# Opening of a two-block transformer kernel: vectors laid out by the host, two modulation chunks multiplied on TensorE, window bias and rope angles moved into the opening

## The reference, cut to what matters

```
cond = silu(c)
mod = cond @ w_mod[l] + b_mod[l]              # 1024 x 9216 per layer
sh1, sc1, g1, sh2, sc2, g2, sh3, sc3, g3 = split(mod, 9)
h = rms_norm(x, norm_g) * (1 + sc1) + sh1     # before each sub-layer
x = x + 0.5 * g1 * swiglu(h, w_gu, w_down)

rel  = pos[query] - pos[key]                  # window attention, 128 wide
bias = rel_bias[t5_bucket(rel)]               # 32 buckets x 6 heads
ang  = pos * 10000 ** (-arange(16) / 16)      # rope of the latent attention
```

## Time and profile before

| what | us |
|---|---|
| median of 3 runs (2005.84 to 2014.0) | 2006.38 |
| the profiled execution, as timed | 2002.22 |
| its span, first to last instruction | 2000.4 |
| PE busy | 1839.9 (92%) |
| DVE busy | 1425.0 (71%) |
| ACT busy | 932.1 (47%) |
| first matmul of the first strip | 66.19 after the start |
| first mixer, from its x_stats to the next | 264.34 to 431.88 |
| the same stage of the second layer | 822.65 to 972.23 |

### The profile page before, as it was taken

One profiled execution on the slowest core, in us unless ns is written; L12 is line 12 of the kernel. 1 busy time (PEld: TensorE's weight loads), 2 busy tenths in 40 slices (PEclk: granted clock), 3 DMA queues, 4 the chain that ended last, 5 costly groups with the idle time before them and its releaser, 6 DMA issues.

```text
span 2000.4 us, 24149 instructions
## 1 busy us (share of the span) xinstructions
PE 1839.9 (92%) x9068; PEld 1490.0 (74%) x9068; DVE 1425.0 (71%) x1956; ACT 932.1 (47%) x1480; POOL 137.2 (7%) x264
## 2 busy tenths in 40 slices
PE   1699986789999999978999999999999999999997
PEld 0577865678887888767788878787878788877886
DVE  5668788767887788676778776567787765567554
ACT  1444344664445444655643364345433544445443
POOL 2011100001110111000011000000111000000000
PEclk9999998889999999986999999999999999999999
DMA  6789823049885898331589865445998563447552
GB/s 243 262 293 340 313 97 127 22 149 329 309 311 197 314 322 324 124 118 42 186 306 336 298 214 187 136 163 171 329 321 299 200 221 128 172 147 271 194 186 86
DMA packets 242299, 439.48 MB, mean 220 GB/s; under 512 B 16201, under 2 KB 156551, under 8 KB 241927
## 3 DMA queue, kind: packets, MB, share of 16 engines
q1 hardware_dynamic: 204810, 304.75, 45.2%
q0 software_dynamic: 36320, 131.13, 17.4%
q10 hardware_dynamic: 1052, 2.06, 0.3%
HBM read 436.79 MB, written 1.09 MB: 219 GB/s over the span
## 4 chain that ended last, share of the span: by engine, by line
PE 73%; DVE 14%; DMA 5%; ACT 5%; issue 3%; SPq 0%; DVEq 0%; ACTq 0%
PE bank L1592 22%; PE bank L1594 21%; PE bank L1593 21%; DVE weights_lo L972 4%; DMA arena<-in_w_ada 2%; DMA arena<-in_w_mod 2%; PE bank L1755 1%; DVE mod_acc L996 1%; DVE arena L1088 1%; DMA weights_raw<-in_w_ffn_gu 1%; DVE x L1152 1%; DVE arena L1146 1%; ACT weights_hi L561 1%; DMA weights_raw<-in_w_ffn_in 1%; DVE hT_lo L1097 1%
## 5 line engine op out<-in xcount | busy, mean ns | idle before, releaser
L972 DVE TENSOR_TENSOR weights_lo<-weights_raw,weights_hi 128x1024 fp32r<-128x1024 f32 (+2 forms) x584 | 672.6, 1199 | 175.6 <-ACT weights_hi L561 175.4
L1592 PE MATMUL bank<-weights_hi,hT_hi 128*128 128x512 f32 x1760 | 699.0, 397 | 31.6 <-DVE hT_lo L1097 20.0
L1594 PE MATMUL bank<-weights_hi,hT_lo 128*128 128x512 f32 x1760 | 686.6, 390 | 0.0
L1593 PE MATMUL bank<-weights_lo,hT_hi 128*128 128x512 f32 x1760 | 685.5, 389 | 0.0
L561 ACT ACTIVATE weights_hi<-weights_raw 128x1024 fp32r<-128x1024 f32 (+2 forms) x584 | 572.1, 1037 | 141.2 <-PE bank L1594 84.0
L1592 PEld LDWEIGHTS bank<-weights_hi,hT_hi 128*128 128x128 f32 x1760 | 332.9, 189 | 115.1 <-issue 27.9
L1594 PEld LDWEIGHTS bank<-weights_hi,hT_lo 128*128 128x128 f32 x1760 | 332.2, 189 | 69.7
L1593 PEld LDWEIGHTS bank<-weights_lo,hT_hi 128*128 128x128 f32 x1760 | 333.3, 189 | 64.0
L996 DVE SCALAR_TENSOR_TENSOR mod_acc<-arena,silu_cond,mod_acc 128x1024 f32<-128x1024 f32 x198 | 254.0, 1283 | 61.8 <-DMA arena<-in_w_mod 28.1
L704 ACT ACTIVATE actT_hi<-bank 128x512 fp32r<-128x512 f32 x66 | 39.5, 599 | 490.7 <-PE bank L1755 490.7
L1592 PE MATMUL bank<-weights_hi,actT_hi 128*128 128x512 f32 (+1 forms) x544 | 214.3, 394 | 7.4 <-DVE weights_lo L972 7.4
(11 more groups left out here) (277 smaller groups left out, 1312.2 us busy)
## 6 DMA issues: line engine op xcount, KB each, us to landing
weights_raw<-in_w_ffn_gu SPq DMA_DIRECT2D x176, 512.0 KB, 5.7
arena<-in_w_mod POOLq DMA_DIRECT2D x144, 512.0 KB, 6.6
weights_raw<-in_w_in SPq DMA_DIRECT2D x112, 512.0 KB, 4.7
arena<-in_w_ada POOLq DMA_DIRECT2D x96, 512.0 KB, 6.2
weights_raw<-in_w_ffn_down SPq DMA_DIRECT2D x88, 512.0 KB, 5.0
weights_raw<-in_w_ffn_in SPq DMA_DIRECT2D x88, 512.0 KB, 5.4
weights_raw<-in_w_ffn_out SPq DMA_DIRECT2D x44, 512.0 KB, 4.6
weights_raw<-in_w_out SPq DMA_DIRECT2D x32, 512.0 KB, 4.4
```

Of the source, the lines that this page charges most:

```text
L972: V.tensor_tensor(wlo[:, slot, 0:width], raw[:, slot, 0:width], whi[:, slot, 0:width].bitcast(F32), ALU.subtract).then_inc(S("lo_done"), 1)
L1592: T.matmul(o, sh, wh, start=start, stop=False)
L1593: T.matmul(o, sh, wl, start=False, stop=False)
L1594: return T.matmul(o, sl, wh, start=False, stop=stop)
```

## The change

- **Host layout.** All vectors come as one array `vectors`, already in columns (384 per partition), and the positions, bias rows and shifted bias rows come as one array `pairs` (334 words per partition). Thirteen row loads, three transposes and three copies go, and so do the fourteen small loads. Constants are reordered so that the first 576 columns hold what the opening needs; the rest is loaded later.
- **Queues.** SP issues the 16 modulation units of chunks 0 and 1 and then the FFN weights. ACT issues `vectors`, `pairs` and the first constants at the start, and the rest of the constants and the five gain vectors after its part of the first strip. POOL issues x, then computes the angles itself (`angles`, 21 arithmetic instructions in a serial chain), then waits for the first four high parts before it loads later modulation units.
- **PE.** Chunks 0 and 1 are multiplied wholly on PE (`mod_unit`, four matmuls a unit). Between the units stand the six `bias_pass` steps (after units 3, 5, 8, 10, 12, 14) and `x_turn(0)` (after unit 9). A bias pass has 192 matmuls with 6 moving columns instead of 64 with 18, the three parts accumulating in PSUM. After the last unit come `x_turn(1)` and four matmuls on zeros.
- **DVE.** It has no modulation units in the opening; the six `bias_reach` and `bias_take` steps (two `reached` buffers, the mask added while reading PSUM) stand between `x_stats` and `mod_store`. The four low parts move behind `scale_cols` into the scaling of x.
- **ACT.** The Sin of the angles is taken before the first high part, and the four high parts are interleaved with the scaling of x.
- **First mixer.** Its bias steps and `window_bias` are gone; its low parts run as in the second layer.

```diff
 def on_pe(m):
-    c0, c1 = next(c for c in [(0, 2)] + MOD_CHUNKS if 8 * c[0] <= m < 8 * c[1])
+    if m < MOD_FIRST_UNITS:
+        return True
+    c0, c1 = next(c for c in MOD_CHUNKS if 8 * c[0] <= m < 8 * c[1])
+BIAS_AFTER = (3, 5, 8, 10, 12, 14)
+X_TURN_AFTER = 9
+TRX_FIRST = (0, 1, 6, 7)
...
 # SP
-            load_rows(sp, 0, 6)
-            sp.dma_start(con[:, :], A["con"]).then_inc(S("const_loaded"), 16)
...
-            sp.wait_ge(S("mod_used"), 12)
+            for m in range(MOD_FIRST_UNITS):
+                mod_load(sp, m)
...
 # POOL
+            def angles():
+                pool.wait_ge(S("pos_loaded"), 16)
+                pool.wait_ge(S("const_loaded"), 16)
+                then(G.tensor_copy(posf_i, pos_i))
...
+                for s in range(2):
+                    part = ang
+                    for c in (c1, c2, c3):
+                        then(G.tensor_scalar(turned_back[:, s], turns[:, s], c, None, ALU.mult))
+                        then(G.tensor_tensor(rope1[:, s], part, turned_back[:, s], ALU.subtract))
+                        part = rope1[:, s]
...
+            pool.dma_start(x[:, :, :], A["x"][0].rearrange("(t p) n -> p t n", p=P)).then_inc(S("x_loaded"), 16)
+            angles()
+            pool.wait_ge(S("hi_done"), RING + PREFETCH)
...
 # ACT
-            load_rows(act, 6, 13)
-            act.wait_ge(S("vec_ready"), 1)
+            act.dma_start(vec[:, :], A["vectors"]).then_inc(S("vec_loaded"), 16)
+            act.dma_start(ar(A_BIAS, 334), A["pairs"]).then_inc(S("pos_loaded"), 16)
+            act.dma_start(con[:, 0:C_FIRST], A["con"][:, 0:C_FIRST]).then_inc(S("const_loaded"), 16)
+            act.wait_ge(S("vec_loaded"), 16)
...
+            def first_phase(a):
+                act.wait_ge(S("angles_ready"), 1)
+                nc.scalar.activation(r1, r1, ACT.Sin).then_inc(S("rope_ready"), 1)
+                act.wait_ge(S("const_loaded"), 16)
+                nc.scalar.activation(table_col[:, :], ident[:, 0:1], ACT.Silu)
+                hi_static(RING, SLOT)
+                act.wait_ge(S("scale_ready"), 1)
+                x_hi(0)
+                x_hi(1)
+                hi_static(RING + 1, SLOT)
+                x_scaled(a, TRX_FIRST, 2)
...
 # DVE
+            def bias_take(q):
+                dve.wait_ge(S("bias_summed"), q + 1)
+                for g in range(4):
+                    c = P * (q // 2) + 32 * g + 16 * (q % 2)
+                    ins = V.tensor_tensor(bias[:, :, c:c + 16], bank[4 + g][:, 0:96].rearrange("p (k h) -> p h k", h=WH),
+                                          con[:, C_MASKW + c:C_MASKW + c + 16].unsqueeze(1).broadcast_to([P, WH, 16]), ALU.add)
+                ins.then_inc(S("bias_taken"), 1)
...
-            dve.wait_ge(S("cond_ready"), 1)
-            mod_units(range(0, 8))
...
+            bias_reach(0)
+            bias_reach(1)
+            bias_take(0)
+            bias_reach(2)
+            bias_take(1)
             x_stats(1, 0)
             x_stats(1, 1)
             x_scale1(1)
+            bias_reach(3)
+            bias_take(2)
             mod_store(0)
-            mod_units(range(8, 16))
-            for u in range(PREFETCH):
-                lo_static(RING + u, SLOT)
+            bias_reach(4)
+            bias_take(3)
+            bias_reach(5)
+            bias_take(4)
+            bias_take(5)
             mod_store(1)
...
 # PE
+            def mod_unit(m):
+                chunk, k = m // 8, m % 8
+                mod_wait(pe, m)
+                parts = modw[:, m % MOD_RING, :].rearrange("p (k r j) -> p r k j", r=4, j=32)
+                for r in range(4):
+                    ins = T.matmul(bank[sum_bank(chunk)][32 * r:32 * (r + 1), 0:256], silc[:, k:k + 1].broadcast_to([P, 32]), parts[:, r],
+                                   start=k == 0, stop=k == 7)
+                ins.then_inc(S("mod_summed" if k == 7 else "mod_read"), 1)
             def bias_pass(q):
...
+                    for part in range(3):
+                        for g in range(4):
+                            r = slice(NBUCKET * g, NBUCKET * (g + 1))
+                            ins = T.matmul(bank[4 + g][:, WH * k:WH * (k + 1)], reached[q % 2][r, k, :], bparts[r, part, :], start=part == 0, stop=part == 2)
...
+                    pe.wait_ge(S("cond_ready"), 1)
+                    for u in range(MOD_FIRST_UNITS):
+                        mod_unit(u)
+                        if u in BIAS_AFTER:
+                            bias_pass(BIAS_AFTER.index(u))
+                        if u == X_TURN_AFTER:
+                            pe.wait_ge(S("const_loaded"), 16)
+                            x_turn(0, TRX_FIRST)
+                    pe.wait_ge(S("bias_taken"), 6)
+                    x_turn(1, TRX_FIRST)
+                    keep_warm(WARM[0])
                     first_strip(n0, strip_banks, None)
+                    pe.wait_ge(S("const_loaded"), 32)
...
                     if m == 0:
-                        dve.wait_ge(S("hlo_done"), tr[0])
-                        window_bias(n0 + 4)
```

More of the change, by code:

```diff
@@ L379, in build, with mod_load, mod_sem, mod_wait @@
         latent_hi, latent_lo = [ahi[:, 0], kvhi], [alo[:, 0], kvlo]
[L381 to L401, removed]
+        def mod_load(eng, m):
+            name, layer, col = mod_source(m // 8)
+            k, was = m % 8, m - MOD_RING
+            if 0 <= was < MOD_FIRST_UNITS and was % 8 < 7:
+                eng.wait_ge(S("mod_read"), was - was // 8 + 1)
+            elif was >= 0 and on_pe(was):
+                eng.wait_ge(S("mod_summed"), was // 8 + 1)
+            else:
+                need(eng, S("mod_used"), taken(was + 1))
+            eng.dma_start(modw[:, m % MOD_RING, :], A[name][layer][k * P:(k + 1) * P, col:col + D]).then_inc(S(mod_sem(m)), 16)
+        def mod_sem(m):
+            return f"first_mod_loaded{m % MOD_RING}" if m < MOD_FIRST_UNITS else f"mod_loaded{m % MOD_RING}"
+        def mod_wait(eng, m):
+            loads = m // MOD_RING + 1
+            eng.wait_ge(S(mod_sem(m)), 16 * (loads if m < MOD_FIRST_UNITS else loads - MOD_FIRST_UNITS // MOD_RING))
         block = ctx.enter_context(nc.Block())
@@ L1303, in _ @@
                     widths = [512, 512, D_IN - 1536]
[L1304 to L1306 removed]
                     for s in range(3):
[L1308 removed]
+                        for u in range(4 if s else 0):
                             lo_static(n0 + 4 * s + u, 2 * widths[s])
@@ L1660, in bias_pass @@
                 for k in range(16):
-                    for g in range(4):
-                        r = slice(NBUCKET * g, NBUCKET * (g + 1))
-                        ins = T.matmul(bank[4 + g][:, 3 * WH * k:3 * WH * (k + 1)], reached[r, k, :], bparts[r].rearrange("p q h -> p (q h)"),
-                                       start=True, stop=True)
+                    for part in range(3):
+                        for g in range(4):
+                            r = slice(NBUCKET * g, NBUCKET * (g + 1))
+                            ins = T.matmul(bank[4 + g][:, WH * k:WH * (k + 1)], reached[q % 2][r, k, :], bparts[r, part, :], start=part == 0, stop=part == 2)
                 ins.then_inc(S("bias_summed"), 1)
@@ L2044 @@
     con, con2 = constants()
-    for name, a in [(k, inputs[k]) for k in INPUTS] + [("con", con), ("con2", con2)]:
+    laid = {k: inputs[k] for k in INPUTS if k not in ("positions", "rel_bias") and k not in [name for _, name in VECTORS]}
+    laid["vectors"], laid["pairs"] = vector_columns(inputs), pair_columns(inputs)
+    for name, a in list(laid.items()) + [("con", con), ("con2", con2)]:
         a = np.ascontiguousarray(a)
```

221 lines of the change are left out of this document (99 added, 122 removed).

## The result

| what | before | after |
|---|---|---|
| median of 19 runs each | 2012.89 | 1994.47 |
| lowest and highest | 2004.07, 2017.43 | 1983.78, 2004.6 |
| the profiled execution, its span | 2002.22, 2000.4 | 1991.88, 1990.1 |
| first matmul of the first strip | 66.19 | 65.06 |
| last matmul of the first strip ends | 78.80 | 78.36 |

After over before is 0.9918, with a 95% interval from 0.9899 to 0.9937: 16 us less (18 by the medians). The forecast was 43 less, 1963 us in a range from 1952 to 1981; even the new median lies above that range. The first stage grew by 5.9 us where 22 less were predicted, and the mixer gave 18.25 of its 21. All later stages are within 2.5 us of before.

What follows compares the result with a forecast made beforehand. The opening was taken as bound by a chain of DMA, DVE modulation units and DMA, the mixer by DVE's bias steps; 22 + 21 = 43 us from 2002.2 gives 1959, as a median 1963, range 1952 to 1981.

Steps and rivals of the forecast that it cites:

- 21 less with bounds 17.7 and 24.1: First mixer: 24.1 us less in its first stretch, up to 6.4 given back in the heads; the middle taken.
- The sum: Opening, three chains added step by step: DMA's last unit at 28 us, PE's at up to 38.4, DVE's store at 39.5.
- units later than one in 1.3 us: Opening: modulation units landing further apart than this were named as a sign that the prediction is wrong.
- I take 1.95: Opening, PE: price in us of one bias pass of 192 matmuls, scaled from 64 in 0.64 us; six passes counted.
- PE lies 1 to 2 us beneath it: Opening: DVE's chain sets the end, and PE's chain is shorter by 1 to 2 us.
- 39.5: Opening: time in us at which store(1) was to end; it ended at 64.04 before.
- 16.4: Us from the end of store(1) to the end of the first strip; 14.8 before.
- The 1 us that the sum gave for ACT's six DMAs: After store(1): ACT issues six DMAs, 0.4 us each, ahead of its next high parts; first strip ends at 57, not 56.
- The rival: Opening: DVE and POOL hinder each other, DVE's chain grows by 6 us, 37 less instead of 43, 1969; chance 0.15.
- the five: Rivals: DVE and POOL hindering 0.15, slow POOL angles 0.08, slower than before 0.03, time given back 0.05, better than sum 0.08.
- the time is given back: Mixer keeps only part, FFN starts with emptier buffers; net 0 to 10 us less, 2000 us; chance 0.05.
- gaps of over 3 us in the first strip for weights: First FFN strip: such gaps were named as a sign that the prediction is wrong.

Runs made afterwards that it cites:

- experiment 3: Changed kernel with bias passes of 64 matmuls of 18 columns and PE's wait for the second constants moved to the first modulation sum; 1974.56 us, 0.9827 of before.
- experiment 10: Changed kernel with only the new opening; bias steps stay in the first mixer, in passes of 64 matmuls; 1993.11 us, one run.
- Experiments 1: Changed kernel with bias passes of 64 matmuls and 18 columns as before, DVE reducing, mask added once at the end; 1979.14 us, 0.9829 of before.
- experiments 4: Changed kernel with only the first of three bias parts multiplied, 64 matmuls of 6 columns a pass; 1984.03 us, one run.
- 6: The kernel with 18-column passes, each matmul cut into three of 6 columns written to their own columns without accumulating, 192 a pass; 1996.73 us, one run.
- experiment 7: Kernel before the change, only its first mixer's bias passes cut into 192 accumulating matmuls, with a copy replacing DVE's reduction; 2021.88 us, one run.
- 8: Changed kernel with modulation units 4 to 15 loaded in only 64 of their 1024 columns; 1986.16 us, one run.
- Experiments 2: Changed kernel with PE's wait for the second constants moved from behind the first strip to the first modulation sum; 2003.06 us, one run.
- experiment 5: Changed kernel with 64-matmul, 18-column bias passes, and second constants and gains issued by ACT after its part of the statistics; 1974.22 us, 0.9834 of before.
- experiment 9: The best version by its marks: experiment 5 with the fourth comparison moved between the two halves of the statistics; 1971.81 us, 0.9810 of before.

## Why the prediction was wrong

**The mixer: right.** 21 less with bounds 17.7 and 24.1; measured 18.25. The gain of the first stretch (24.4) and the 6.4 given back in the heads both came as their rows said; layer 0 got layer 1's clock. That this end of the range came is chance as far as the runs show: in experiment 3 the same heads ran at 0.82 in 42.64 us.

**DMA in the opening: not the bound, as said, but slower than its sum.** The first constants let DVE start at 11.76 (11.5), and PE lost 3.9 us to late units. The sum had the last unit there at 28 if PE keeps up. In experiment 10 PE keeps up, waits for units 12 times, and begins the last one at 32.70:

```profile
31.28 1.08 PE L1672 MATMUL bank<-arena,silu_cond 128*32 128x256 f32 x8 [2.77 <-DMA arena<-in_w_mod]
32.70 1.08 PE L1672 MATMUL bank<-arena,silu_cond 128*32 128x256 f32 x8 [0.33 <-DMA arena<-in_w_mod]
```

From the first unit at 5.55 that is one in 1.8 us, and units later than one in 1.3 us were a sign named in advance. It would have cost nothing by itself, since 32.7 is still before the 38.4 of the sum.

**DVE: each duration right.** The comparison is 2.28 us, a take 0.75 (0.8), the statistics 25.97 to 30.4 (4.4), as the timeline shows:

```profile
20.81 2.28 DVE L1061 TENSOR_TENSOR arena<-arena 128x2048 bf16<-128x2048 f32 x1
...
43.60 2.28 DVE L1061 TENSOR_TENSOR arena<-arena 128x2048 bf16<-128x2048 f32 x1
48.37 0.75 DVE L1069 TENSOR_TENSOR window_bias<-bank,con 128x96 f32<-128x96 f32 x4 [2.48 <-PE bank L1687]
59.79 0.75 DVE L1069 TENSOR_TENSOR window_bias<-bank,con 128x96 f32<-128x96 f32 x4 [10.67 <-PE bank L1687]
```

But DVE didn't set the end. It waited 10.67 us for the last pass alone.

**PE: the failed step.** "If columns decide it stays 0.64, if the count decides it is 1.92. I take 1.95", and from it "PE lies 1 to 2 us beneath it". As a busy time this is right: 192 matmuls without a gap took 1.7 to 1.9 us. As a price of the pass it is wrong. The row it came from was one pass of 64, 128 instructions, half a block, in a stretch that used few instructions otherwise; what was multiplied by three was a burst shorter than a block. In a row, passes run at the rate at which blocks come. From the first to the last matmul of a pass it took between 3.3 us (the second) and 9.6 us (the last, 50.07 to 59.69), and 31.7 us for the six together, where the sum had 6 x 1.95 = 11.7. The bounds of 0.64 and 1.92 both came from the same burst, so they couldn't hold the truth. `mod_store(1)` ended at 61.9 and not at 39.5, 22.4 us later, and 20.5 of these stand in the seven gaps. Experiments 1 and 4 take the count away and the gaps go; 6 keeps the count without accumulation, and they stay; 7 takes it elsewhere, where gaps of 6.4 us come with it and the stretch is 10.6 us longer; 8 takes half the traffic away and keeps 17.3. The section of the Trainium skill that the prediction cited ("TensorEngine Tiling (Array Packing)", "Instruction Overhead"), a constant overhead per matmul, agrees with the trace in that 6 and 18 columns cost the same in a burst, 10 ns each, and says nothing of the supply.

**After the store: right up to the strip's end, then short.** The first matmul came 3.2 us after it as forecast, the strip ended 16.5 after (16.4). The 1 us that the sum gave for ACT's six DMAs was the wrong form of the right worry: the strip ended without that 1 us, but the constants among them came 3.69 us late for PE. Behind this wait PE restarted at the low clock:

```profile
78.36:82.04 3.68, 0.00 (x0) 0.00 (x0) 3.37 (x5) 2.55 (x4) 0.00 (x0) 1.00 1.01 399
82.04:86.60 4.56, 4.56 (x13) 3.62 (x14) 4.23 (x5) 0.00 (x0) 1.52 (x3) 0.63 0.34 105
```

13 matmuls took 4.56 us at 0.63 where 25 took 5.30 at 1.00 before, about 1.8 us more. From the strip's end to x_stats it was 191.9 us, against 185.5 before: 3.7 the wait, 1.8 the clock, 1 the turns. The sum had carried this stage over unchanged. Experiments 2 and 3 show that taking this wait away alone brings nothing at x_stats, since the weights are then late.

**POOL: right, and the lock is there on one side.** The angle chain ended at 25, before the 30 asked for, and ACT never waited for it. Most of its instructions took 0.24 to 0.40 us (0.35 taken); three did not:

```profile
14.00 2.24 POOL L537 TENSOR_SCALAR arena<-arena 128x64 f32<-128x64 f32 x1
16.33 2.08 POOL L541 TENSOR_SCALAR arena<-arena 128x32 f32<-128x32 f32 x1
...
19.53 0.29 POOL L541 TENSOR_SCALAR arena<-arena 128x32 f32<-128x32 f32 x1
...
20.94 2.30 POOL L541 TENSOR_SCALAR arena<-arena 128x32 f32<-128x32 f32 x1
```

Each of the three begins beside one of the first three comparisons (two in 13.72 to 18.25, one in 20.81 to 23.09) and ends within 0.25 us of its end, while comparisons stayed at 2.28. The rival had DVE pay 6 us; POOL paid 6, off the path. The rule cited there from the Trainium skill ("SBUF — State Buffer", section "SBUF: two separate sides"), an exclusive lock held for a whole instruction, is what POOL sees when DVE holds it; no comparison was lengthened here. Experiment 10, whose opening has no comparisons, bears it out. The same 21 instructions run from 11.33 to 18.86 there, none longer than 0.40 us, and the first of the three takes

```profile
13.56 0.37 POOL L537 TENSOR_SCALAR arena<-arena 128x64 f32<-128x64 f32 x1
```

**The rivals.** None of the five named the supply of instructions. The one nearest in size ("the time is given back", 0.05, 2000 us) had the total about right by a mechanism that took no part: the mixer kept its gain. Of the signs named in advance for a wrong forecast, gaps of over 3 us in the first strip for weights, only a relative came: 3.7 us for constants behind it, the smaller part of the miss.

**Left open.** What bounds the rate of blocks was not measured: whether the packet's way through the DMA engines, or PE's sequencer; how many blocks PE has ahead at a time; and whether the granted clock of 0.50 to 0.60 in the later passes lengthens it. The best version still takes 201.5 us from its first matmul to x_stats, against 198.15 before. In experiment 5, part of that stands at the FFN's end at a clock of 0.75 (0.86 in the last 12 us of experiment 9); neither this clock nor the rest was traced to a cause.

## What to carry to other kernels

Count instructions, not only busy time: a duration read from one burst of tiny matmuls is no price for a row of such bursts, and three times the matmuls with a third of the columns each left PE idle for 20.5 us here, beyond the some 8 us by which they keep it busy (8.4 in experiment 7). In a profile, idle time named `issue` inside one unrolled loop, at multiples of 128 matmuls with their weight loads, beside an instruction queue that moves many packets, is the sign. And where an opening is held by three chains, the one taken out uncovers the next: here constants, then weights, so judge a change by the next phase's start and not by the wait that it removes.

## What the runs showed of the hardware

- Blocks of 256 instructions came no closer than 3 us or so in the quiet mixer of experiment 7 and on average every 4.45 us in the passes of the changed kernel; 128 small matmuls with their weight loads use a block up in 1.18 us.
- In a burst of 64, a matmul of 32 rows in four row groups costs 10 ns with 6 and with 18 columns alike (experiments 4 and 1).
- The heads of the first mixer, the same instructions, ran at a granted clock of 0.64 in some profiles and 0.82 in others, 49.15 and 42.64 us (after and experiment 3).
- The scatter between runs, some 10 us either way, has one visible source. One long stage of the second block takes 212.7 us in the profile of after, and 223.6 in that of experiment 3, with the same work:

```profile
1153.37:1366.03 212.66, 205.23 (x957) 168.36 (x956) 134.47 (x181) 100.90 (x135) 1.07 (x2) 0.98 0.51 171
```
```profile
1134.40:1358.00 223.60, 216.19 (x957) 177.01 (x957) 134.39 (x181) 101.08 (x136) 1.06 (x2) 0.93 0.48 163
```

The granted clock is 0.98 in the one and 0.93 in the other. Three of the eleven new profiles have the long form (experiments 2, 3 and 4), so that the time of a single run can't judge less than 10 us; marks ahead of that stage are not touched by it.
